# Linear-attention and recurrence projections in three split fp32r products, values of four heads in one pass, first recurrence tile ahead of the last head

## The chip, the cores and the metric

The program runs on one core of a Trainium2 chip. A core has a matrix engine (TensorE, PE; the loading of its weights is PEld), a vector engine (VectorE, DVE), an activation engine (ScalarE, ACT), a general engine (GpSimd, POOL) and a queue engine (SyncE, SP) that issues transfers. Each runs its own list of instructions; they wait for one another by semaphores. The metric is the device time of one execution in microseconds.

## The reference, cut to what matters

The program computes two blocks of a network for 512 positions of width 1024, in fp32. The change lies in the mixer of the first block, in its linear-attention heads and its gated recurrence:

```
def hgrn2_chunked(q, k, v, log_f):      # 8 heads of 128; S_t = diag(f_t) S_{t-1} + k_t v_t^T ; o_t = S_t^T q_t
...
def hybrid_mixer(u, lb, w_in, b_in, ...):
    proj = u @ w_in + b_in
    hq, hf, hi, hg, lx, lg, ca, cb, g_a, g_b, g_c = jnp.split(proj, cuts, axis=-1)
    q = jax.nn.silu(hq.astype(f32)).reshape(hshape)
    z = hf.astype(f32).reshape(hshape)
    f = lb_h + (1.0 - lb_h) * jax.nn.sigmoid(z)
    k = (1.0 - lb_h) * jax.nn.sigmoid(-z)
    v = hi.astype(f32).reshape(hshape)
    o_hg = hgrn2_chunked(q, k, v, jnp.log(f))
    y_hg = rmsnorm(o_hg, hg_norm)... * jax.nn.silu(hg)
    xb = causal_dwconv(lx, lru_conv_w, lru_conv_b)       # 4 taps
    ...                                                  # two gates from xb, a linear scan over positions
    y_lru = h.astype(u.dtype) * jax.nn.gelu(lg)
    cu = ca * jax.nn.sigmoid(cb)
    cu = causal_dwconv(cu, cv_dw_w, cv_dw_b)             # 31 taps
    y_cv = jax.nn.silu(layernorm(cu, cv_ln_g, cv_ln_b))
    merged = sigmoid(g_a) * (y_hg @ w_branch[0]) + sigmoid(g_b) * (y_lru @ w_branch[1]) + sigmoid(g_c) * (y_cv @ w_branch[2])
    return merged @ w_out
```

## The kernel before, in words

All activations lie with channels on the 128 partitions and the 512 positions along a row: xn is the normalised input of the mixer, 8 tiles of 128 channels. Weights come from memory as slabs of 128 x 1024 (512 KB) in one fixed order, by SyncE, into a ring of four; a slab's place is filled again once TensorE has counted it in slab_used.

A product is made in one of two ways. Plain (L515, L524, L532, L792): one fp32 matmul for each of the 8 input tiles, straight from ring and xn. Split (product, L220 to L222): weights and input are each the sum of a high part (what fp32r holds) and a low part, and low x high, high x high and high x low are added in PSUM. The high part of a slab is a copy on ScalarE (split_hi, L205, into whi), the low part a subtraction on GpSimd (split_lo, L210, in place in the ring as ring_r). The input's high part is xh1 (ScalarE), its low part xn_r (VectorE, x_lo_tile L233 or L926). The feed-forward parts and the merge are split; linear attention and recurrence are plain.

Linear attention (hgrn) goes head by head, each engine with a function of its own, over a hardware loop (Fori). Per head TensorE projects the query into bank 0, the output gate into bank 1, z into bank 2 and the values, position tile by position tile, into bank 3 (L532, with the bias by a one-row matmul L530). Its order is proj(h+1), inner part of h (hgrn_intra: L563 transposes, L555 eight score products, L571 states, L578 and L580 output, L583 sum of squares), query(h+2). ScalarE: sigmoid of the gate (L612), absolute value, exponentials and logarithms of z (L614 to L632), copy L634, sigmoid of the next query (L606), then square L638, logarithm L640 and exponential L642 for the norm. VectorE: gate L662, z L664, values copy L666, decays L670 to L684, level differences L690 and L691, masked queries and keys L699 and L700, score copies L707 and L712, states, next query L656, norm L728 and L730. Bank 1 is free for the next head's gate when L662 has run, and L662 waits for a sigmoid that waits for L730 of the head before.

The recurrence stage (lru) goes over 8 channel tiles. Per tile TensorE makes four projections (L792, banks 0 to 3) and two gate products (L802); VectorE does 4 taps (L888, L891), the convolution's input (L893), the gelu (L897 to L901), 31 taps (L913, L914, L920, two running sums in turn), the sum L922, and the scan (L928 to L932). Here 2 steps of the taps are independent of each other, while L891, L907 to L909 and L928 to L932 each wait for the step before. In the last tile ScalarE and VectorE also make xh1 and xn_r for the merge (L855, L926), and GpSimd splits the first merge slabs.

After it comes a layer norm (L813 mean, L939, L942, L870, L819) and the merge.

Of the kernel before, what the change touches and what calls it, by code (L numbers as in the profile page):

```python
# [7 lines left out]
ALU = mybir.AluOpType  # L8
# [6 lines left out]
P = 128  # L15
# [33 lines left out]
PARTS = [("ffn1_in", 2 * FT), ("ffn1_out", FT), ("hgrn", 4 * HEADS), ("lru", 4 * DT), ("merge", 6 * DT),  # L49
# [13 lines left out]
for _n, _c in PARTS:  # L63
    if _n in ("ffn1_in", "ffn1_out", "ffn2_in", "ffn2_out", "merge", "mix_out", "in2", "v2", "merge2", "out2"):
        SPLIT_AT[_n] = _at
        _at += _c
# [31 lines left out]
def hybrid_block_kernel(nc, stream, par, x_t, vbias, gate_w, masks, ctx_t, rpb, router_w, lora, experts, spill, xs_dram, ys_dram, out):  # L98
    ctx = ExitStack()
    with ctx:  # L100
# [46 lines left out]
        WHI = {"in2": whi2, "v2": whi2, "merge2": whi3, "out2": whi3}  # L147
        y_hg, y_lru, y_cv, merged = (big[:, i, :, :] for i in range(4))
# [325 lines left out]
        hq, hgl, hz, hlf, hk, hB, hqd, hkd, hv_tok, hkdT, hsc, hst, ho, hl1, he1, hEB = (WU(21 + n) for n in range(16))  # L474
        hst3 = hst[:, 0:3 * P].rearrange("p (c v) -> p c v", v=P)
        hi = Steps(sem("hgrn_pe"), "kdt s0 s1 kv s2 s3 s4 s5 s6 s7 o ss", 12)
        ha = Steps(sem("hgrn_act"), "sgg az e l1 sn e1 l2 EB Ekd E0 E1 kdT sgq osq lnss rstd", 16)
        hv = Steps(sem("hgrn_dve"), "gh z V lf t1 zc lf2 kh B dk " + " ".join(f"dr{i} dl{i}" for i in range(7))
                   + " qd kd " + " ".join(f"qm{i} km{i}" for i in range(7))
                   + " c0 c1 S1 S2 S3 c2 c3 c4 c5 c6 c7 qh y1 y2")  # L480
        hv.base = len(hv.names)
        hz_ready = sem("hgrn_zeros")
        vb_in = sem("vb_in")
        vb = shared[0:1, 11 * P:11 * P + D]
# [3 lines left out]
        xs_zeroed = sem("xs_zeroed")  # L488

# [5 lines left out]
        def hgrn_pool(pool):  # L495
# [7 lines left out]
            pool.memset(kl, 0.0).then_inc(hz_ready, 1)  # L503

        first_head = lambda h: isinstance(h, int) and h == 0

        def hgrn_query(pe, h, j0, i):

            if not first_head(h):
                pe.wait_ge(hv.sem, hv.at(h - 2, "qh"))  # L510
            w = use_slab(pe, "hgrn", j0, i, 4)
            for k in range(DT):
                if first_head(h):
                    pe.wait_ge(xn_ready, DT + k + 1)
                ins = pe.matmul(psum[:, 0, :], w[:, k, :], xn[:, k, :], start=k == 0, stop=k == DT - 1)  # L515
            ins.then_inc(slab_used, 1)

        def hgrn_proj(pe, h, j0, i):

            for n, (bank, freed) in enumerate(((1, "gh"), (2, "z"))):  # L520
                pe.wait_ge(hv.sem, hv.at(h - 1, freed))
                w = use_slab(pe, "hgrn", j0 + 1 + n, i, 4)
                for k in range(DT):
                    ins = pe.matmul(psum[:, bank, :], w[:, k, :], xn[:, k, :], start=k == 0, stop=k == DT - 1)  # L524
                ins.then_inc(slab_used, 1)

# [31 lines left out]
        def hgrn_intra(pe, h):  # L558
            pe.wait_ge(hv.sem, hv.at(h, "kd"))
# [39 lines left out]
        def hgrn_act(act):  # L599
# [8 lines left out]
            def head(h, last):  # L608
# [26 lines left out]
                if not last:  # L635
                    query(h + 1, 1)
# [2499 lines left out]
```

## Time and profile before

| what | us |
|---|---|
| median of 3 runs | 3611.16 (3605.09 to 3613.73) |
| span of the profiled execution, first to last instruction | 3608.5 |
| the same execution's time around the span | not listed apart; the median of the runs is 2.7 above the span |
| linear attention, first product to last L730 | 418.8 to 809.8 |
| recurrence stage, first product to last L932 | 809.9 to 1105.8 |
| mean granted TensorE clock over the span | 0.916 |

The engines' busy time is to be read by stage: from 500 to 768 us (six heads) TensorE is busy 248.0 of 268, VectorE 156.8, ScalarE 144.2, GpSimd 0. From 843 to 1069 (seven recurrence tiles) VectorE is busy 213.1 of 226. In a row of the order of time, a group of instructions stands with its start, its length from first start to last end, and in brackets how long the engine was idle before it and what ended that.

### The profile page before, as it was taken

The page shows a single profiled execution, that of the slowest core. Times are in us where ns is not written, and L with a number is a line of the kernel's source. Part 1 is how long each engine was busy: PE and PEld are TensorE (multiplying, and loading weights), DVE is VectorE, ACT ScalarE, POOL GpSimd, SP SyncE. Part 2 cuts the span into 40 slices and gives each one's busy share as a digit, 9 for nine tenths or more (in the row PEclk, how much of TensorE's full clock was granted, in tenths as well). Part 3 has the DMA queues.
Part 4 walks back from the last instruction along what each step waited for, and adds up shares of the span by engine and source line. Part 5 has one row for each costly group of instructions (what it writes and reads, how often), then busy time and mean ns, then how long its engine had stood idle before and what let it go on. Part 6 is the DMA issues. An engine that isn't in the chain of part 4 may idle for free.

```text
span 3608.5 us, 57604 instructions
## 1 busy us (share of the span) xinstructions
PE 3203.3 (89%) x22992; PEld 2391.1 (66%) x22992; DVE 1692.7 (47%) x2566; ACT 1336.9 (37%) x1755; POOL 766.0 (21%) x438
## 2 busy tenths in 40 slices
PE   7999999969967999899998999976777699599996
PEld 5887666644425887787833786756777477378885
DVE  2110155556996332311014403456666431489996
ACT  4432245553333322443122222222222232278884
POOL 4444200000004443444401231001111244200001
PEclk9999999989988999999999996557999889799998
DMA  2222511102211222222364121000000022399996
GB/s 103 95 95 89 210 52 46 47 24 74 74 50 53 94 94 87 77 93 87 97 230 141 53 85 38 12 9 3 4 4 4 2 88 94 129 362 412 412 412 270
DMA packets 106923, 397.17 MB, mean 110 GB/s; under 512 B 11680, under 2 KB 11696, under 8 KB 106240
## 3 DMA queue, kind: packets, MB, share of 16 engines
q1 hardware_dynamic: 95040, 347.42, 26.7%
q0 software_dynamic: 8400, 35.15, 2.6%
q10 hardware_dynamic: 3312, 12.06, 0.8%
q8 instruction: 139, 2.28, 0.3%
q14 instruction: 32, 0.26, 0.0%
HBM read 361.55 MB, written 33.03 MB: 109 GB/s over the span
## 4 chain that ended last, share of the span: by engine, by line
PE 66%; DVE 13%; issue 5%; ACT 2%; DMA 1%; DVEq 1%; POOL 0%; ACTq 0%; SPq 0%
PE psum L222 9%; PE psum L221 9%; PE psum L220 9%; PE psum L1760 6%; PE psum L2616 3%; PE psum L2617 3%; PE psum L2618 3%; PE psum L524 3%; PE psum L1429 2%; PE psum L1110 2%; DVE mem L920 2%; PE psum L532 2%; PE psum L1409 2%; PE psum L1790 1%; PE psum L792 1%
## 5 line engine op out<-in xcount | busy, mean ns | idle before, releaser
L210 POOL TENSOR_TENSOR ring_r<-ring,whi 128x1024 fp32r<-128x1024 f32 x247 | 600.0, 2439 | 1018.5 <-ACT whi L205 1018.5
L205 ACT ACTIVATE whi<-ring 128x1024 fp32r<-128x1024 f32 x247 | 255.6, 1055 | 529.6 <-DMA ring<-stream 529.4
L222 PE MATMUL psum<-xn_r,whi 128*128 128x512 f32 x1024 | 406.2, 397 | 0.0
L1760 PE MATMUL psum<-mem 64*64 64x64 f32 x9664 | 264.5, 234 | 87.9 <-DVE mem L2075 60.2
L1760 PEld LDWEIGHTS psum<-mem 64*64 64x64 f32 x9664 | 249.7, 147 | 100.9 <-DVE mem L2075 67.3
L2553 DVE TENSOR_TENSOR er_r<-er,eh 128x1024 fp32r<-128x1024 f32 x268 | 309.4, 1220 | 1.1 <-ACT eh L2541 0.5
L220 PE MATMUL psum<-ffn_xh,ring_r 128*128 128x512 f32 x704 | 279.7, 397 | 18.9 <-DVE xn_r L233 18.9
L2541 ACT ACTIVATE eh<-er 128x1024 fp32r<-128x1024 f32 x268 | 268.4, 1070 | 41.6 <-DMA er<-experts 40.9
L221 PE MATMUL psum<-ffn_xh,whi 128*128 128x512 f32 x704 | 281.3, 400 | 0.0
L792 PE MATMUL psum<-xn,ring 128*128 128x512 f32 x512 | 224.6, 599 | 8.5 <-DVE mem L730 4.3
L222 PEld LDWEIGHTS psum<-xn_r,whi 128*128 128x128 f32 x1024 | 193.9, 189 | 45.2
L220 PE MATMUL psum<-xh,ring_r 128*128 128x512 f32 x504 | 205.1, 407 | 9.1 <-DVE resid_r L1166 8.6
L221 PE MATMUL psum<-xh,whi 128*128 128x512 f32 x504 | 202.1, 401 | 0.0
L455 DVE TENSOR_TENSOR gu<-gu,psum 128x512 f32<-128x512 f32 x44 | 30.3, 688 | 358.4 <-ACT gu L434 358.4
L792 PEld LDWEIGHTS psum<-xn,ring 128*128 128x128 f32 x512 | 98.0, 192 | 134.0 <-issue 128.9
L220 PEld LDWEIGHTS psum<-ffn_xh,ring_r 128*128 128x128 f32 x704 | 132.9, 189 | 56.6 <-issue 19.7
L920 DVE SCALAR_TENSOR_TENSOR mem<-mem,pv 128x512 f32 (+1 forms) x232 | 157.1, 752 | 0.0
L221 PEld LDWEIGHTS psum<-ffn_xh,whi 128*128 128x128 f32 x704 | 133.4, 189 | 31.2
L220 PE MATMUL psum<-hid_hi,ring_r 128*128 (+1 forms) x352 | 143.9, 409 | 7.7 <-DVE hid_lo L459 7.7
L2616 PE MATMUL psum<-er_r,xbh 128*128 128x512 f32 x368 | 146.4, 398 | 3.4 <-DVE er_r L2553 2.0
L2618 PE MATMUL psum<-eh,xbl 128*128 128x512 f32 x368 | 144.4, 392 | 0.0
L2617 PE MATMUL psum<-eh,xbh 128*128 128x512 f32 x368 | 144.3, 392 | 0.0
(510 smaller groups left out, 6129.4 us busy)
## 6 DMA issues: line engine op xcount, KB each, us to landing
ring<-stream SPq DMA_DIRECT2D x359, 512.0 KB, 3.5
er<-experts SPq DMA_DIRECT2D x276, 512.0 KB, 8.0
xs_dram<-zero_row POOLq DMA_DIRECT2D x1, 12288.0 KB, 38.7
xs<-xs_dram SPq DMA_DIRECT2D x23, 512.0 KB, 8.1
ys_dram<-y_t ACTq DMA_DIRECT2D x23, 512.0 KB, 6.6
mem<-rpb POOLq DMA_DIRECT2D x8, 512.0 KB, 4.3
resid<-x_t SPq DMA_DIRECT2D x1, 2048.0 KB, 7.9
spill<-resid POOLq DMA_DIRECT2D x1, 2048.0 KB, 10.3
```

Of the source, the lines that this page charges most:

```text
L205: act.activation(WHI.get(part, whi)[:, (SLAB_AT[part] + j) % RING, :, :], w, ACT.Copy).then_inc(w_hi, 1)
L210: pool.tensor_tensor(ring_r[:, s, :, :], ring[:, s, :, :], f(WHI.get(part, whi)[:, s, :, :]), ALU.subtract).then_inc(w_lo, 1)
L220: pe.matmul(bank, lo[:, b, :], x_hi_, start=start, stop=False, skip_group_check=True)
L221: pe.matmul(bank, hi[:, b, :], x_hi_, start=False, stop=False, skip_group_check=True)
L222: return pe.matmul(bank, hi[:, b, :], x_lo_, start=False, stop=stop, skip_group_check=True)
L792: ins = pe.matmul(psum[:, bank, :], w[:, k, :], xn[:, k, :], start=k == 0, stop=k == DT - 1)
L1760: ins = pe.matmul(psum[o, bank, n * L:(n + 1) * L], lhs(n)[r], rhs(n)[r], start=i == 0 if start is None else start, stop=i == len(terms) - ...
L2541: act.activation(eh[:, SLOT[kind] + j, :], er[:, SLOT[kind] + j, :], ACT.Copy).then_inc(e_hi, 1)
L2553: dve.tensor_tensor(er_r[:, at, :], er[:, at, :], f(eh[:, at, :]), ALU.subtract).then_inc(e_lo_dve, 1)
L2616: pe.matmul(bank, x_hi_, lo_[:, cols], start=start, stop=False, skip_group_check=True)
L2617: pe.matmul(bank, x_hi_, hi_[:, cols], start=False, stop=False, skip_group_check=True)
L2618: return pe.matmul(bank, x_lo_, hi_[:, cols], start=False, stop=stop, skip_group_check=True)
```

## The change

1. The query, gate and z projections of all heads and the four projections of every recurrence tile become split products. Their slabs get a high and a low part (ScalarE L205, GpSimd L210 before; L209 and L214 in the new file), in a buffer whi_h of their own. xh1 and xn_r are made right at the mixer's norm, between the steps of norm_dve, and kept through both stages.
2. The values of four heads are made in one pass, split, with the weights as the moving side: two passes hv0 and hv1 of 96 matmuls into banks 4 to 7, one before head 0's projections and one after. VectorE adds the bias (values), for all 128 partitions. The slab order of the stream follows.
3. On ScalarE the gate's sigmoid of head h+1 stands right behind the query's sigmoid, with two buffers in turn (hgl), followed by an explicit load of the table set with logarithm and exponential. The next head's weight copies follow, ahead of the square.
4. The first recurrence tile's four projections (lru_first) stand before the last head's inner part.
5. In the recurrence loop ScalarE copies and GpSimd subtracts the next tile's four slabs (ahead).
6. The low parts for the merge leave the last recurrence tile; buffers move (y_cv, merged, y_cv_lo, mrg_lo).

```diff
-PARTS = [("ffn1_in", 2 * FT), ("ffn1_out", FT), ("hgrn", 4 * HEADS), ("lru", 4 * DT), ("merge", 6 * DT),
+PARTS = [("ffn1_in", 2 * FT), ("ffn1_out", FT), ("hv0", 4), ("hq0", 3), ("hv1", 4),
+         ("hgrn", 3 * HEADS - 3), ("lru", 4 * DT), ("merge", 6 * DT),
...
@@ hgrn_pool, after the two memsets
+            for j in range(4):
+                split_lo(pool, "hv0", j)
+            for j in range(3):
+                split_lo(pool, "hq0", j)
+            for j in range(4):
+                split_lo(pool, "hv1", j)
+            for h in range(1, HEADS):
+                for n in range(3):
+                    split_lo(pool, *head_slab(h, n))
+            for j in range(4):
+                split_lo(pool, "lru", j)
...
+        def hgrn_product(pe, bank, h, n):
+            w = use_split(pe, *head_slab(h, n))
+            for k in range(DT):
+                ins = product(pe, psum[:, bank, :], w, k, xh1[:, k, :], xn_r[:, k, :], k == 0, k == DT - 1)
+            ins.then_inc(slab_used, 1)
...
+        def hgrn_values(pe, g):
+            for s in range(4):
+                w_high, w_low = use_split(pe, f"hv{g}", s)
+                for c in range(4):
...
+                        pe.matmul(psum[:, 4 + c, :], xh1[:, k, at], w_low[:, cols, :], start=k == 0, stop=False, skip_group_check=True)
+                        pe.matmul(psum[:, 4 + c, :], xh1[:, k, at], w_high[:, cols, :], start=False, stop=False, skip_group_check=True)
+                        ins = pe.matmul(psum[:, 4 + c, :], xn_r[:, k, at], w_high[:, cols, :], start=False, stop=k == DT - 1,
...
@@ hgrn_pe
-            with pe.Fori(0, HEADS - 2) as h:
-                hgrn_proj(pe, h + 1, 4, h)
+            hgrn_values(pe, 0)
+            hgrn_query(pe, 0)
+            hgrn_proj(pe, 0)
+            hgrn_values(pe, 1)
+            hgrn_query(pe, 1)
+            for h in range(HEADS - 2):
+                hgrn_proj(pe, h + 1)
                 hgrn_intra(pe, h)
+                hgrn_query(pe, h + 2)
+            hgrn_proj(pe, HEADS - 1)
             hgrn_intra(pe, HEADS - 2)
+            lru_first(pe)
             hgrn_intra(pe, HEADS - 1)
@@ hgrn_act
+            def gate(h, count):
                 proj_done(act, h, 2)
-                act.wait_ge(hv.sem, hv.at(h - 1, "y2"))
-                act.activation(hgl, psum[:, 1, :], ACT.Sigmoid, bias=b(3)).then_inc(s, 1)
+                act.wait_ge(hv.sem, hv.at(h - 2, "y2"))
+                act.activation(hgl[h % 2], psum[:, 1, :], ACT.Sigmoid, bias=b(3, h)).then_inc(s, count)
...
                 if not last:
                     query(h + 1, 1)
+                    gate(h + 1, 1)
+                    act.preload_act_table_set("natural_log_exp_and_others")
+                if h < HEADS - 2:
+                    for n in range(3):
+                        split_hi(act, *head_slab(h + 2, n))
+                if h == HEADS - 2:
+                    for j in range(4):
+                        split_hi(act, "lru", j)
...
@@ lru_pool
-            with pool.Fori(0, DT) as j:
+            with pool.Fori(0, DT - 1) as j:
                 pool.wait_ge(lp.sem, lp.at(j - 1, "i"))
                 pool.dma_start(gwt, gate_w[:, j, :, :]).then_inc(gw_in, 16)
+                for n in range(4):
+                    split_lo(pool, "lru", 4 + n, j, 4)
...
@@ lru_act, channels
+                ahead = (lambda n: split_hi(act, "merge", n)) if last else (lambda n: split_hi(act, "lru", 4 + n, j, 4))
+                ahead(0)
+                ahead(1)
                 done(4)
...
+                ahead(2)
...
+                ahead(3)
...
@@ lru_dve, channels
-                if last:
-                    for k in range(DT):
-                        dve.wait_ge(x_hi, INPUT_AT["mix"] + k + 1)
-                        dve.tensor_tensor(xn_r[:, k, :], xn[:, k, :], f(xh1[:, k, :]), ALU.subtract).then_inc(x_lo, 1)
...
-            norm_dve(dve, 1, "norm_mix", xn)
+            norm_dve(dve, 1, "norm_mix", xn, xh1, "mix")
```

ScalarE in one head of linear attention, before (L612 sigmoid of the gate, L614 to L624 the functions of z):

```order
L612 ACT_TABLE_LOAD [waits hgrn_dve]
L612 ACTIVATE mem<-psum,pv 128x512 [waits slab_used]
L614 ACTIVATE mem<-mem 128x512 [waits hgrn_dve]
L616 ACT_TABLE_LOAD
L616 ACTIVATE mem<-mem 128x512 [waits hgrn_act]
L618 ACT_TABLE_LOAD
L618 ACTIVATE mem<-mem,ones 128x512 [waits hgrn_act]
L620 ACT_TABLE_LOAD
L620 ACTIVATE mem<-mem 128x512 [waits hgrn_dve]
L622 ACTIVATE mem<-mem 128x512 [waits hgrn_dve]
L624 ACT_TABLE_LOAD
L624 ACTIVATE mem<-mem,ones,lb 128x512 [waits hgrn_act]
```

ScalarE from the sigmoid of the next query to the first functions of z, now (L642 and L647 the two sigmoids, L209 weight copies, L687 to L691 the norm, L652 and L654 what L614 and L616 were):

```order
L642 ACT_TABLE_LOAD [waits hgrn_pe]
L642 ACTIVATE mem<-psum,pv 128x512 [waits slab_used]
L647 ACTIVATE mem<-psum,pv 128x512 [waits hgrn_dve,slab_used]
L679 ACT_TABLE_LOAD
L209 ACTIVATE whi_h<-ring 128x1024 [waits slab_in0]
L209 ACTIVATE whi_h<-ring 128x1024 [waits slab_in1]
L209 ACTIVATE whi_h<-ring 128x1024 [waits slab_in2]
L687 ACTIVATE mem<-psum 128x512 [waits hgrn_pe]
L689 ACTIVATE mem<-psum,eps 128x512 [waits hgrn_pe]
L691 ACTIVATE mem<-mem 128x512 [waits hgrn_act]
L652 ACTIVATE mem<-mem 128x512 [waits hgrn_dve]
L654 ACTIVATE mem<-mem 128x512 [waits hgrn_act]
```

The table loads between the functions of z are gone, and one load and three weight copies of 128 x 1024 now stand ahead of the square.

GpSimd between the first feed-forward and the merge, before (two memsets, then those of the recurrence stage and its loop, which only fetches gate weights):

```order
L502 MEMSET mem 128x3584 [waits resid_ready]
L503 MEMSET mem 128x3584
L772 MEMSET mem 128x3 [waits hgrn_dve]
L773 MEMSET mem 128x30
L774 UNCONDITIONAL_BRANCH
L774 ISA
L776 ISA [waits lru_pe]
```

and now (the same memsets; L214 is the weight subtraction, 36 of them in linear attention, and from L843 the recurrence loop):

```order
L513 MEMSET mem 128x3584 [waits resid_ready]
L514 MEMSET mem 128x3584
L214 TENSOR_TENSOR ring_r<-ring,whi_h 128x1024 [waits w_hi] x36
L841 MEMSET mem 128x3 [waits hgrn_dve]
L842 MEMSET mem 128x30
L843 UNCONDITIONAL_BRANCH
L843 ISA
L845 ISA [waits lru_pe]
L845 DMA mem<-gate_w 128x256
L213 ISA
L214 TENSOR_TENSOR ring_r<-ring,whi_h 128x1024 [waits w_hi]
```

36 subtractions moved into linear attention, and the recurrence loop has four in each of its seven rounds.

## Rows read from the trace of the kernel before

**Rows 1.** The page, part 1: busy us (share) and instructions of each engine.
```profile
PE 3203.3 (89%) x22992; PEld 2391.1 (66%) x22992; DVE 1692.7 (47%) x2566; ACT 1336.9 (37%) x1755; POOL 766.0 (21%) x438
```

**Rows 2.** Busy time by stage; columns: stretch, length, engines, PEclk, DMA share, GB/s.
```profile
843.00:1069.00 226.00, 203.91 (x471) 88.84 (x470) 213.14 (x323) 80.17 (x99) 3.77 (x7) 0.97 0.21 69
```

**Rows 3.** Order of time (start us, length us, what), GpSimd, VectorE, TensorE, linear attention.
```profile
414.89 3.08 POOL L503 MEMSET mem<- 128x3584 f32 x1
...
417.89 5.39 DVE L367 SCALAR_TENSOR_TENSOR xn<-resid,pv,std 128x512 f32<-128x512 f32 x8
...
418.79 9.08 PE L515 MATMUL psum<-xn,ring 128*128 128x512 f32 x16 [5.14 <-DVE xn L367]
...
481.21 0.60 PE L563 MATMUL psum<-ident,mem 128*128 128x128 f32 x4
...
498.70 0.69 DVE L730 TENSOR_TENSOR mem<-mem 128x512 f32 x1
...
766.76 0.69 DVE L730 TENSOR_TENSOR mem<-mem 128x512 f32 x1
```

**Rows 4.** Order of time, TensorE: split products, then two plain slabs.
```profile
37.08 0.40 PE L221 MATMUL psum<-ffn_xh,whi 128*128 128x512 f32 x1
...
37.31 0.39 PE L222 MATMUL psum<-xn_r,whi 128*128 128x512 f32 x1
...
427.71 13.90 PE L524 MATMUL psum<-xn,ring 128*128 128x512 f32 x32
```

**Rows 5.** Order of time in one head, ScalarE, TensorE, VectorE.
```profile
592.51 0.63 ACT L614 ACTIVATE mem<-mem 128x512 f32<-128x512 f32 x1 [1.59 <-DVE mem L664]
...
593.16 1.28 ACT L616 ACT_TABLE_LOAD   x1
...
615.24 0.41 DVE L700 TENSOR_TENSOR mem<-mem 128x256 f32<-128x256 f32 x1
...
628.99 7.03 PE L515 MATMUL psum<-xn,ring 128*128 128x512 f32 x16
```

**Rows 6.** Order of time at the end of head 7, VectorE and ScalarE; last, one group of ScalarE.
```profile
793.85 0.68 DVE L707 COPY mem<-psum 128x512 f32<-128x512 f32 x1
...
801.13 0.72 DVE L712 COPY_PREDICATED mem<-ident,psum 128x512 f32<-128x512 uint32 x1 [0.18 <-DVE mem L712]
...
803.77 0.60 ACT L638 ACTIVATE mem<-psum 128x512 f32<-128x512 f32 x1 [12.67 <-PE psum L580]
...
808.34 0.75 DVE L728 SCALAR_TENSOR_TENSOR mem<-psum,pv,mem 128x512 f32<-128x512 f32 x1 [6.49 <-ACT mem L642]
...
L606 ACT ACTIVATE mem<-psum,pv 128x512 f32<-128x512 f32 x8 | 5.5, 687 | 0.1
```

**Rows 7.** Order of time in the recurrence stage, VectorE; last ScalarE.
```profile
842.60 0.75 DVE L893 SCALAR_TENSOR_TENSOR mem<-psum,pv,mem 128x512 f32<-128x512 f32 x1 [17.25 <-ACT mem L835]
...
912.17 0.69 DVE L901 SCALAR_TENSOR_TENSOR mem<-mem 128x512 f32<-128x512 f32 x1 [0.69 <-ACT mem L842]
...
1068.37 0.74 DVE L893 SCALAR_TENSOR_TENSOR mem<-psum,pv,mem 128x512 f32<-128x512 f32 x1
...
1075.56 1.99 ACT L205 ACTIVATE whi<-ring 128x1024 fp32r<-128x1024 f32 x2
```

**Rows 8.** Single lines, duration ns min/median/max, and the stretch of GpSimd beside them.
```profile
L210 POOL TENSOR_TENSOR ring_r<-ring,whi x66: 2333/2411/2436, 22.5 to 389.4; 128x1024 fp32r<-128x1024 f32 x66
...
1076.68 10.49 POOL L210 TENSOR_TENSOR ring_r<-ring,whi 128x1024 fp32r<-128x1024 f32 x2 [36.24 <-ACT whi L205]
...
L210 POOL TENSOR_TENSOR ring_r<-ring,whi x2: 2779/5261/7743, 1076.7 to 1084.4; 128x1024 fp32r<-128x1024 f32 x2
...
L909 DVE SCALAR_TENSOR_TENSOR mem<-mem x8: 691/692/2711, 860.0 to 1082.3; 128x512 f32<-128x512 f32 x8
...
L920 DVE SCALAR_TENSOR_TENSOR mem<-mem,pv x29: 739/740/2833, 1072.3 to 1096.9; 128x512 f32<-128x512 f32 x29
...
L942 DVE TENSOR_TENSOR mem<-mem x8: 1526/1760/2832, 1108.1 to 1119.7; 128x512 f32<-128x512 f32 x8
```

More of the change, by code:

```diff
@@ L577, in hgrn_intra @@
                 s = slice(c * P, (c + 1) * P)
-                ins = pe.matmul(psum[:, 4, s], hv_tok[:, s], hsc[:, s], start=True, stop=c == 0)
+                ins = pe.matmul(psum[:, 4, s], value(c), hsc[:, s], start=True, stop=c == 0)
                 if c:
@@ L642, in head @@
                 act.activation(hl1, hl1, ACT.Exp, scale=-0.5).then_inc(s, 1)
-            query(0, 4)
-            with act.Fori(0, HEADS - 1) as h:
-                head(h, False)
-            head(HEADS - 1, True)
+            split_hi(act, "hv0", 0)
+            split_hi(act, "hv0", 1)
+            x_hi_act(act, 1, xh1)
+            split_hi(act, "hv0", 2)
+            split_hi(act, "hv0", 3)
+            for n in range(3):
+                split_hi(act, *head_slab(0, n))
+            split_hi(act, "hv1", 0)
+            query(0, 1)
+            split_hi(act, "hv1", 1)
+            gate(0, 4)
+            act.preload_act_table_set("natural_log_exp_and_others")
+            split_hi(act, "hv1", 2)
+            split_hi(act, "hv1", 3)
+            for h in range(HEADS):
+                head(h)
         def hgrn_dve(dve):
@@ L729, in head @@
                 own("y1")
-                dve.tensor_tensor(y_hg[:, h, :], hl1, hgl, ALU.mult).then_inc(s, 1)
+                dve.tensor_tensor(y_hg[:, h, :], hl1, hgl[h % 2], ALU.mult).then_inc(s, 1)
+            values(0)
             query(0, 3)
-            with dve.Fori(0, HEADS - 1) as h:
-                head(h, False)
-            head(HEADS - 1, True)
+            for h in range(HEADS):
+                head(h)
         lxp = work[:, 0:520]
@@ L795, in lru_proj, with lru_first @@
                     lru_gates(pe, gates)
+        def lru_first(pe):
+            for bank, head, freed in ((0, HEADS - 2, "qh"), (1, HEADS - 1, "gh"), (2, HEADS - 1, "z"), (3, HEADS - 1, "z")):
+                pe.wait_ge(hv.sem, hv.at(head, freed))
+                w = use_split(pe, "lru", bank)
+                for k in range(DT):
+                    ins = product(pe, psum[:, bank, :], w, k, xh1[:, k, :], xn_r[:, k, :], k == 0, k == DT - 1)
+                ins.then_inc(slab_used, 1)
         def lru_gates(pe, j):
@@ L850, in channels @@
                 act.activation(la_t, lr, ACT.Exp, scale=c).then_inc(s, 1)
-                if last:
-                    split_hi(act, "merge", 0)
-                    split_hi(act, "merge", 1)
-                    for k in range(DT):
-                        act.activation(xh1[:, k, :], xn[:, k, :], ACT.Copy).then_inc(x_hi, 1)
                 act.wait_ge(lv.sem, lv.at(j, "w"))
@@ L3072, in lay_out @@
     mix = k_slabs(i["w_in_mix"][0]).reshape(11, DT, P, SLAB, P)
-    parts.append(mix[[0, 3, 1, 2]].transpose(1, 0, 2, 3, 4).reshape(-1, P, SLAB, P))
+    heads = mix[[0, 3, 1]].transpose(1, 0, 2, 3, 4).reshape(-1, P, SLAB, P)
+    values = i["w_in_mix"][0][:, 2048:3072].reshape(4, 2, P, 2, 4, P).transpose(3, 0, 2, 1, 4, 5).reshape(2, 4, P, SLAB, P)
+    parts.extend([values[0], heads[0:3], values[1], heads[3:]])
     parts.append(mix[[4, 5, 6, 7]].transpose(1, 0, 2, 3, 4).reshape(-1, P, SLAB, P))
```

131 lines of the change are left out of this document (69 added, 62 removed).

## The prediction

> **What bounds the kernel now.** I read the page first: over the whole span TensorE is busy 89%, VectorE 47%, GpSimd 21% [rows 1]. That average hides the two stages that the change touches, so I went on to the busy time by stage, then to the order of time of each engine inside one head and inside one channel tile, and last to single instructions of GpSimd and VectorE. The reader is to see four things.
>
> Linear attention runs in a loop in which TensorE closes the cycle. The last VectorE step of a head (L730) ends at 499.4 us for head 0 and 767.4 for head 6 [rows 3], so a head takes 268.1 / 6 = 44.7 us, and TensorE is at work nearly all of it: three projections, the values product and the inner part of the previous head stand in one row.
>
> The recurrence stage is bound by VectorE: from 843 to 1069 us it is busy 213.1 of 226, GpSimd 3.8 [rows 2]. The step that takes the convolution input (L893) is at 842.60 for tile 0 and 1068.37 for tile 7 [rows 7]; in a steady tile VectorE waits about 0.7 us (L901).
>
> The only idle stretch of VectorE is at the start of that stage: L893 of tile 0 waits 17.3 us for the projections [rows 7].
>
> GpSimd and VectorE hinder each other. A weight subtraction on GpSimd takes 2.41 us when VectorE is quiet (66 of them in the first feed-forward). In the last recurrence tile there are two, and they took 7.74 and 2.78 us, while one L909 took 2.71 instead of 0.69 and one L920 2.83 instead of 0.74: 2.0 and 2.1 us lost on VectorE [rows 8]. The first subtraction was issued in a gapless row of L920 and did not get through for 5 us; it came in where a VectorE step waits for the one before it (L907 to L909).
>
> **Part by part.** All sums are against the profiled span of 3608.5 us; the median of the runs shown is 2.7 us above it, and I add that at the end.
>
> *Cheaper projections.* Plain: two slabs (16 products) in 13.90 us, or 0.86 us each. Split: one matmul each 0.23 us (37.08 to 37.31), three to a product, 0.70 us, so 5.6 us a slab instead of 6.9 [rows 4]. Of a head's 44.7 us three plain slabs are 20.8; the other 24 are the values and the inner part. The values (32 narrow products with their bias rows, the columns of one more slab and some on top) are an estimated 9.6 of them; they now go in two passes of 96 matmuls, 22.4 us each, for all heads, outside the loop. What is left to TensorE in a head is 3 x 5.6 and an inner part of 14: 31 us. That is not what is to be had, since another chain comes to the front.
>
> *Start of linear attention.* TensorE began at 418.79, as soon as the first normalised tile was there [rows 3]. Now it needs that tile's low part and the first split weight slab. GpSimd's two memsets end at 418.0, VectorE's row of 8 L367 begins at 417.89 [rows 3], and with the 8 low parts put between them it runs gapless to about 428 (8 x 0.67 from the row of 5.39, and 8 x 0.6 for the low parts, an estimate from L730, a step of the same kind and size, 0.69 less 0.09 of overlap). By rows 8 the subtraction waits for its end: TensorE starts near 430 (+11.5). If GpSimd gets in at once it is 422.7 (+4): that is the other end. From there to head 0's inner part (L563, 481.21 before, 62.4 us after the start) now stand 14 slabs, 14 x 5.6 = 78.3 us, plus about 2 us in which TensorE starts slower after a pause (before, the first slab took 9.08 instead of 7.03 us [rows 3, 5]), plus 4 us in which head 1's first slab waits for its subtraction behind VectorE's gapless row, plus 1.5 for the pause that this makes: 86. The inner part starts 35 us later.
>
> *A head's new cycle.* From VectorE's L730: gate and z steps 1.5; then L614 to the last L700, 592.51 to 615.65 = 23.1, less three table loads of 1.28 on the path that the preload takes away (L616, L618, L624) = 19.4; the score copies 793.85 to 801.85 = 8.0 [rows 6] (head 7, where TensorE had nothing else to do); then on ScalarE a sigmoid table load 1.28, two sigmoids 1.3, the preload 1.3, three weight copies 3.0 (two take 1.99 [rows 7]) before the square (L638) can run: it starts 6.1 us after the last score copy instead of 1.9; then square, sum, logarithm, exponential and two VectorE steps, 6.2 us before [rows 6] less two loads that partly lay beside TensorE: 4.9. Sum 1.5 + 19.4 + 8.0 + 6.1 + 4.9 = 39.9. GpSimd's three subtractions begin after the first weight copy and last 7.2 us; the third still runs when L730 (two operands in SBUF) is issued: 1.1 us. 41.0 a head, 3.7 less than 44.7; TensorE (31) is then hidden. Against y of head 0 (+35, and a tail 4 us longer than before by the same items: +39), six heads give back 22: +17 at the end of head 6. Head 7, with the first recurrence tile (22.4 us of TensorE) filling the wait of head 7's own chain, gives back 4: +13.
>
> The Trainium skill (ScalarE: Activation LUTs, "What ACT_TABLE_LOAD costs") gives a switch of sets 1.28 us of load and 1.38 us of drain. The load agrees; the trace does not show the drain: L616's load starts at 593.16, right behind L614, which ends at 593.14 [rows 5]. By the page a head would gain some 4 us more, 28 us in all.
>
> *First recurrence tile ahead.* L893 of tile 0 came 32.8 us after linear attention's end (809.8). Now its products are done: table load and copy 2.5, three filter taps 3.8, sigmoid meanwhile: 7.1. Gain 25.7: the sum stands at -13.
>
> *Weight splits in the recurrence stage.* 28 slabs (tiles 1 to 7) are now copied on ScalarE and subtracted on GpSimd inside the stage that VectorE bounds. ScalarE's 4 x 1.0 us lie in waits of 5 to 10 us a tile and cost nothing. Each subtraction costs VectorE 2.05 us [rows 8] or, if it falls into the one idle 0.7 us, less: 4 x 2.05 - 0.7 = 7.5 us a tile, seven tiles 52.5. Below, nothing (all of them find gaps); above, 4 x 2.8 = 11. I take 7.5, since the only two subtractions seen in this very loop cost that. The sum so far is +40. Cheaper projections gain nothing here; TensorE goes from 29 to 24 us in a tile of 39.
>
> The Trainium skill (SBUF — State Buffer, "Who interferes with whom") states that a VectorE instruction with two SBUF inputs and a GpSimd instruction that reads SBUF exclude each other for a whole instruction. The trace agrees: L909 and L920 have two inputs in SBUF and were held for 2.0 and 2.1 us. Without such a lock the whole sum would be -15, which is the first rival below.
>
> *Last tile and merge.* The eight low parts leave VectorE's last tile (4.9 us), but TensorE's mean product there did not wait for them. The high parts start 5 us earlier, and fewer of L942's eight steps (1.76 us instead of 0.69 beside GpSimd [rows 8]) are hit: -2. The moved buffers and the wider bias transfer cost nothing.
>
> Sum: 39 (start) - 22 - 4 - 25.7 + 52.5 - 2 = +37.8 us. Span 3646, run 3649 us; I say 3648, as the items are not sharper than that.
>
> **Rivals.**
> *The lock does not bite.* Subtractions find the seams between VectorE's steps and the recurrence tile stays at 31.8. For: GpSimd's other 66 ran undisturbed; against: there VectorE was mostly idle, and the two in this loop did bite. Then 37.8 - 52.5 = -15, and with a start at 422.7 a further -8: 3588 to 3599 us, faster. It decides if a subtraction costs VectorE under 0.7 us.
> *Starved GpSimd.* The subtractions wait 5 us each as the first did, TensorE waits for the slabs, gates come late: 4 x 5.3 = 21 us of GpSimd a tile would still fit, but two waits in a row in front of the gates would give tiles near 46: +50 more, 3698.
> *TensorE still closes the head.* If the head chain were shorter than I read, heads would fall to 31: another -60 us, 3588. Against: every item of the 41 has its row.
> *Half and half.* Some subtractions hit and some not: about 3620, no change.
>
> **Chances.** Forecast 0.62 (its own range 3625 to 3675), lock without effect 0.20, starved 0.08, TensorE-bound heads 0.03, half and half 0.07. A run of this kernel tells about 0.3% (11 us) from no change. Slower 0.70, same 0.08, faster 0.22. Range 3588 to 3690.
>
> **What would show it.** Single L920 and L891 near 2.8 us, four GpSimd subtractions a tile and a tile distance of 39 us confirm the main term; a distance of 32 refutes it and the forecast. TensorE's first product at 430 or 423 settles the start. Head distance 41, with VectorE's longest wait on the exponential behind the weight copies, confirms the head chain; 31 to 36 says that I put too much on ScalarE. The convolution input of tile 0 should come 7 us after linear attention's end.

## The result, and the profile after

The kernel became slower, by less than 1%: 3639.2 us (median of 4 runs, 3631.3 to 3644.2) against 3610.9 us for the kernel before (median of 4). The ratio is 1.0085, with a 95% interval of 1.0067 to 1.0104. The profiled execution has a span of 3642.3 us, 33.8 more than before. The forecast was 3648 us, +37.8 in the span. The profiled execution is the slowest of the four: in the medians the difference is 28.4 us.

Busy time of the engines over the whole span, then the two stages by stretch (length, PE, PEld, DVE, ACT, POOL, PEclk, DMA share, GB/s):

```profile
PE 3151.6 (87%) x23056; PEld 2478.8 (68%) x23056; DVE 1753.7 (48%) x2566; ACT 1327.4 (36%) x1763; POOL 930.8 (26%) x502
...
532.00:780.00 248.00, 194.01 (x973) 158.70 (x973) 153.74 (x361) 107.79 (x127) 43.33 (x20) 0.91 0.12 39
828.00:1107.00 279.00, 195.77 (x694) 145.27 (x692) 269.38 (x324) 106.72 (x126) 85.90 (x35) 0.82 0.18 56
```

TensorE has 52 us less to do than in [rows 1], and the kernel is slower all the same. In the recurrence stage it is now busy for 70% of the time, while VectorE is busy for 269 of 279 us: the stage [rows 2] went from 226 to 279 us. VectorE computes nothing new there; its steps only last longer.

The start of linear attention, in order of time (start us, length us):

```profile
417.33 5.08 POOL L214 TENSOR_TENSOR ring_r<-ring,whi_h 128x1024 fp32r<-128x1024 f32 x2
...
417.28 6.34 DVE L371 SCALAR_TENSOR_TENSOR xn<-resid,pv,std 128x512 f32<-128x512 f32 x3
...
424.37 0.77 PE L559 MATMUL psum<-ring_r,xh 128*128 128x512 f32 x1 [11.33 <-DVE xn_r L237]
...
512.20 0.60 PE L596 MATMUL psum<-ident,mem 128*128 128x128 f32 x4
```

GpSimd's first two subtractions got in at once, and it was VectorE that waited: three normalisation steps took 6.34 us, where eight took 5.39 before [rows 3]. TensorE therefore began at 424.4, 5.6 us later than before, and the inner part of head 0 31 us later.

The heads: the last VectorE step of a head, L800 (it was L730), then ScalarE's chain in front of it in head 2, and L800 of head 6:

```profile
L800 DVE TENSOR_TENSOR mem<-mem x8: 693/936/2292, 532.4 to 817.7; 128x512 f32<-128x512 f32 x8
...
603.86 1.28 ACT L642 ACT_TABLE_LOAD   x1 [11.55 <-PE psum L585]
605.15 0.69 ACT L642 ACTIVATE mem<-psum,pv 128x512 f32<-128x512 f32 x1
605.74 0.68 ACT L647 ACTIVATE mem<-psum,pv 128x512 f32<-128x512 f32 x1
606.43 1.28 ACT L679 ACT_TABLE_LOAD   x1
607.73 2.95 ACT L209 ACTIVATE whi_h<-ring 128x1024 fp32r<-128x1024 f32 x3
610.58 0.57 ACT L687 ACTIVATE mem<-psum 128x512 f32<-128x512 f32 x1
...
780.56 2.29 DVE L800 TENSOR_TENSOR mem<-mem 128x512 f32<-128x512 f32 x1
```

Head 0 ends at 532.4 and head 6 at 780.6, so a head takes 248.2 / 6 = 41.4 us instead of 44.7 (41.9 the first, 41.2 to 41.4 the others). All of linear attention still ends 8.6 us later than before (last step at 817.7 against 809.1), since head 0 ends 33.7 us later. The square L687 starts 6.76 us after the start of the last score copy (603.82), 6.0 after its end: a load, two sigmoids, a load and three weight copies stand in front of it.

The recurrence stage: the convolution input L971 (it was L893), one steady tile, and the end of the last tile:

```profile
828.13 0.74 DVE L971 SCALAR_TENSOR_TENSOR mem<-psum,pv,mem 128x512 f32<-128x512 f32 x1
...
911.69 0.74 DVE L971 SCALAR_TENSOR_TENSOR mem<-psum,pv,mem 128x512 f32<-128x512 f32 x1
...
926.19 17.03 DVE L998 SCALAR_TENSOR_TENSOR mem<-mem,pv 128x512 f32<-128x512 f32 x16
...
947.32 4.40 DVE L969 SCALAR_TENSOR_TENSOR mem<-mem,pv 128x512 f32<-128x512 f32 x3
951.64 0.74 DVE L971 SCALAR_TENSOR_TENSOR mem<-psum,pv,mem 128x512 f32<-128x512 f32 x1
...
929.99 8.05 POOL L214 TENSOR_TENSOR ring_r<-ring,whi_h 128x1024 fp32r<-128x1024 f32 x3 [13.01 <-ACT whi_h L209]
948.34 2.83 POOL L214 TENSOR_TENSOR ring_r<-ring,whi_h 128x1024 fp32r<-128x1024 f32 x1 [10.31 <-ACT whi_h L209]
...
1106.97 0.74 DVE L971 SCALAR_TENSOR_TENSOR mem<-psum,pv,mem 128x512 f32<-128x512 f32 x1
...
1134.78 0.69 DVE L1006 SCALAR_TENSOR_TENSOR mem<-mem 128x512 f32<-128x512 f32 x1
```

Tile 0 has its input at 828.1, 14.5 us earlier than in [rows 7]; tile 7 at 1107.0, 38.6 later. A tile takes 40.0 us instead of 31.8. In it GpSimd runs three subtractions beside a row of 16 filter taps, which takes 17.03 us (10.68 in a kernel without them, below), and one beside a row of three, which takes 4.40 (2.54): 6.35 + 1.86 = 8.2 us, the whole difference.

### The profile page after: what moved, and what is told of

Read it like the earlier page. It is cut to its first block, busy times and chain, and to the rows that moved or that the text cites. A ratio compares the mean times of both kernels' runs of the same rounds, so it can differ in the third digit from the quotient of the medians.

```text
span 3642.3 us, 57318 instructions
## 1 busy us (share of the span) xinstructions
PE 3151.6 (87%) x23056; PEld 2478.8 (68%) x23056; DVE 1753.7 (48%) x2566; ACT 1327.4 (36%) x1763; POOL 930.8 (26%) x502
## 4 chain that ended last, share of the span: by engine, by line
PE 72%; DVE 15%; issue 7%; ACT 3%; DMA 1%; POOL 1%; DVEq 0%; ACTq 0%; SPq 0%; POOLq 0%
PE psum L224 13%; PE psum L226 13%; PE psum L225 13%; PE psum L1834 6%; PE psum L2690 4%; PE psum L2691 3%; PE psum L2692 3%; PE psum L1503 2%; PE psum L1184 2%; DVE mem L998 2%; PE psum L1483 2%; PE psum L1864 1%; PE psum L585 1%; PE psum L1492 1%; DMA ring<-stream 1%
## 5 line engine op out<-in xcount | busy, mean ns | idle before, releaser
L214 POOL TENSOR_TENSOR ring_r<-ring,whi 128x1024 fp32r<-128x1024 f32 x247 | 595.1, 2421 | 999.6 <-ACT whi L209 999.6
L224 PE MATMUL psum<-xh,ring_r 128*128 128x512 f32 x952 | 405.8, 426 | 57.2 <-POOL ring_r L214 38.8
L209 ACT ACTIVATE whi<-ring 128x1024 fp32r<-128x1024 f32 x247 | 255.6, 1055 | 531.1 <-DMA ring<-stream 530.9
L2615 ACT ACTIVATE eh<-er 128x1024 fp32r<-128x1024 f32 x268 | 268.3, 1071 | 41.0 <-DMA er<-experts 40.3
L214 POOL TENSOR_TENSOR ring_r<-ring,whi_h 128x1024 fp32r<-128x1024 f32 x64 | 171.2, 2697 | 409.2 <-ACT whi_h L209 409.2
L224 PEld LDWEIGHTS psum<-xh,ring_r 128*128 128x128 f32 x952 | 189.0, 199 | 118.1 <-POOL ring_r L214 47.2
L998 DVE SCALAR_TENSOR_TENSOR mem<-mem,pv 128x512 f32 (+1 forms) x232 | 190.9, 897 | 0.0
L225 PE MATMUL psum<-xh,whi_h 128*128 128x512 f32 x448 | 189.2, 422 | 0.0
L226 PE MATMUL psum<-xn_r,whi_h 128*128 128x512 f32 x448 | 186.7, 417 | 0.0
```

The lines of the kernel that those rows point to most:

```text
L209: act.activation(WHI.get(part, whi)[:, (SLAB_AT[part] + j) % RING, :, :], w, ACT.Copy).then_inc(w_hi, 1)
L214: pool.tensor_tensor(ring_r[:, s, :, :], ring[:, s, :, :], f(WHI.get(part, whi)[:, s, :, :]), ALU.subtract).then_inc(w_lo, 1)
L224: pe.matmul(bank, lo[:, b, :], x_hi_, start=start, stop=False, skip_group_check=True)
L225: pe.matmul(bank, hi[:, b, :], x_hi_, start=False, stop=False, skip_group_check=True)
L226: return pe.matmul(bank, hi[:, b, :], x_lo_, start=False, stop=stop, skip_group_check=True)
L998: dve.scalar_tensor_tensor(half_sum, cup[:, t:t + T], tap("cv_w", t), half_sum, ALU.mult, ALU.add).then_inc(s, 1)
```

## The experiments

Each ratio is to the kernel before, with its 95% interval. A time "after" is of the changed kernel.

**Recurrence tiles 1 to 7 plain again.**

```diff
-                for n in range(4):
-                    split_lo(pool, "lru", 4 + n, j, 4)
...
-                    ins = product(pe, psum[:, bank, :], w, k, xh1[:, k, :], xn_r[:, k, :], k == 0, k == DT - 1)
+                    ins = pe.matmul(psum[:, bank, :], w[:, k, :], x_whole[:, k, :], start=k == 0, stop=k == DT - 1)
...
+            for k in range(DT):
+                pool.tensor_tensor(x_whole[:, k, :], f(xn_r[:, k, :]), f(xh1[:, k, :]), ALU.add).then_inc(x_sum, 1)
```

> Tiles 1 to 7 of the recurrence stage multiply the plain fp32 weights again, with no weight splits (28 copies on ScalarE and 28 subtractions on GpSimd gone); GpSimd puts the input together again once (8 additions beside head 7). Theory (the subtractions hold VectorE, about 8 us a tile): the distance of two tiles falls from 40.0 to 31.8 us and the kernel by some 53 us, to 3586 (3580 to 3594, where the 8 additions hit VectorE). Rival (the tile became longer because of the slower TensorE clock or of the order of the slabs): plain products need 29 us of TensorE a tile instead of 24, and the distance stays above 36: 3610 or more.

3592.2 us (7 runs, 3580.4 to 3596.0), ratio 0.995 (0.9933 to 0.9967). Span 3590.4, 51.9 less than after. VectorE in order of time, tile 2 to tile 3, and the starts of L975 (the convolution input) in all tiles:

```profile
907.21 10.68 DVE L1002 SCALAR_TENSOR_TENSOR mem<-mem,pv 128x512 f32<-128x512 f32 x16
...
921.99 2.54 DVE L973 SCALAR_TENSOR_TENSOR mem<-mem,pv 128x512 f32<-128x512 f32 x3
...
L975 DVE SCALAR_TENSOR_TENSOR mem<-psum,pv,mem x8: 744/745/747, 824.0 to 1055.4; 128x512 f32<-128x512 f32 x8
```

The tile is back at 31.8 us, and tile 7's input comes 51.6 us earlier. The rival (slower TensorE clock, order of slabs) is out: plain products need more of TensorE, and the tile is shorter. Linear attention ends as after (817.3), and tile 0's input now comes 6.7 us behind it instead of 10.4: the splits for tile 1 had already held tile 0's first taps.

**Four more subtractions in the kernel before, and four memsets in their place.**

```diff
+                for n, step in enumerate(("lx", "lx", "sb", "sqg")):
+                    pool.wait_ge(la.sem, la.at(j, step))
+                    pool.wait_ge(extra, 4 * j + n)
+                    pool.tensor_tensor(spare, other, other, ALU.subtract).then_inc(extra, 1)
...
(second kernel)
+                    pool.memset(spare, 0.0).then_inc(extra, 1)
```

> The kernel before with four more GpSimd subtractions (128x1024 fp32, result unused) in each of the recurrence tiles 0 to 6, and nothing else: no weight copies, the products plain. Theory (the subtractions alone make the tile longer): the distance of two tiles goes from 31.8 to 39.3 to 40.0 us, the kernel takes some 55 us more, 3665. Rival (part of the 8.2 us a tile is due to ScalarE's copies, or to slabs that come late): the distance stays at 32 to 36, 3610 to 3640.

> The same places as in the kernel with four more subtractions, but each is a memset of 128x1024 fp32: GpSimd writes SBUF and reads nothing. Theory (what holds VectorE is a GpSimd instruction that reads SBUF): distance 31.8 us, time as before, 3609. Rival (any long GpSimd instruction on SBUF holds VectorE): 36 to 40 us, 3640 to 3665.

With subtractions 3651.6 us, ratio 1.0113 (1.0097 to 1.013); with memsets 3614.6, ratio 1.0001 (0.9987 to 1.0015). First the kernel with subtractions: taps, the second row with its subtraction, the next tile's input, GpSimd beside the taps; all starts of the input. Then GpSimd and the starts of the input with memsets.

```profile
938.00 15.59 DVE L930 SCALAR_TENSOR_TENSOR mem<-mem,pv 128x512 f32<-128x512 f32 x16
...
957.72 4.27 DVE L901 SCALAR_TENSOR_TENSOR mem<-mem,pv 128x512 f32<-128x512 f32 x3
...
940.83 6.91 POOL L783 TENSOR_TENSOR mem<-resid 128x1024 f32<-128x1024 f32 x3 [12.38 <-ACT mem L842]
...
L903 DVE SCALAR_TENSOR_TENSOR mem<-psum,pv,mem x8: 743/747/751, 843.2 to 1108.5; 128x512 f32<-128x512 f32 x8
```

```profile
L783 POOL MEMSET mem<- x28: 952/952/1049, 821.9 to 1034.3; 128x1024 f32 x28
...
L903 DVE SCALAR_TENSOR_TENSOR mem<-psum,pv,mem x8: 744/745/751, 842.6 to 1068.1; 128x512 f32<-128x512 f32 x8
```

Subtractions alone, with TensorE's work and ScalarE's left as they were, lengthen a tile by 6.6 us (4.9 in the row of 16, 1.7 in the row of three) and the seven distances by 39.6. The direction is the theory's, the size is not: I expected 7.5 to 8.2 a tile and 3665 us. These subtractions read one buffer twice and last 2.15 us (median), those of the changed kernel read two and last 2.8 beside taps; the former hold a row of taps for 1.6 us each (4.91 / 3), the latter for 2.1 (6.35 / 3). The two kinds also write different types, and which of these differences makes the price is not shown. The 28 memsets cost nothing (31.8 us a tile). They are shorter too, 0.95 us, but even at half the price of a subtraction they would have shown as 3 us a tile, and no filter tap beside one lasts over 0.75 us. So for steps with two inputs in SBUF, as the taps are, it is the reading of SBUF that counts.

**The subtractions on VectorE.**

```diff
+                ahead = (lambda n: None) if last else (lambda n: split_lo(dve, "lru", 4 + n, j, 4))
...
+                ahead(0)
+                ahead(1)
                 own("cu")
```

> The changed kernel with the 28 subtractions of the recurrence tiles on VectorE itself instead of GpSimd. Theory: VectorE pays its own time, about 1.3 us each (twice the 0.69 of a 512-column step with two SBUF inputs) instead of 2.05 us of being held: 31.8 + 4 x 1.3 - 0.7 = 36.3 us a tile, 7 x 3.7 = 26 us less, 3613. Rival (copies on ScalarE come too late for the fixed places and VectorE waits for them): 38 us or more a tile, 3625 or more.

3653.2 us, ratio 1.0112 (1.0093 to 1.0131); a tile takes 41.0 to 41.6 us, and the last distance is 44.9 (35.5 with the subtractions on GpSimd). VectorE's two first subtractions of a tile, and its steps behind the first taps:

```profile
910.32 2.36 DVE L214 TENSOR_TENSOR ring_r<-ring,whi_h 128x1024 fp32r<-128x1024 f32 x2
...
927.25 0.69 DVE L982 TENSOR_TENSOR mem<-mem 128x512 f32<-128x512 f32 x1 [2.84 <-ACT mem L928]
...
929.90 0.70 DVE L984 TENSOR_TENSOR mem<-mem 128x512 f32<-128x512 f32 x1 [1.95 <-ACT mem L933]
```

My theory falls. The subtraction costs what I said (1.2 us), but it now stands in VectorE's order behind the convolution input, the gate products stand behind two split slabs on TensorE, and VectorE waits 2.84 + 1.95 us for the gates: 4 x 1.2 + 4.8 = 9.6 us a tile, more than the 8.2 on GpSimd. The rival's time came true, but not its cause: VectorE waits in front of none of the 28 subtractions, so ScalarE's copies are never late.

**Tile 0 behind head 7.**

```diff
-            lru_first(pe)
             hgrn_intra(pe, HEADS - 1)
...
             pe.wait_ge(hv.sem, hv.end(HEADS))
+            lru_first(pe)
```

> The projections of recurrence tile 0 stand behind head 7 again instead of ahead of its inner part. Theory (the move alone is worth the idle time of VectorE at the start of the stage): 22.4 us of TensorE come back onto the path, less what head 7 gains without them (about 2): 3660. Rival (they delay head 7 as much as they save): no change, 3640.

3657.3 us, ratio 1.0136 (1.0118 to 1.0153), 18 us more than after; 3660 was expected. End of head 7 and tile 0's input:

```profile
816.39 0.69 DVE L799 TENSOR_TENSOR mem<-mem 128x512 f32<-128x512 f32 x1
...
843.64 0.75 DVE L971 SCALAR_TENSOR_TENSOR mem<-psum,pv,mem 128x512 f32<-128x512 f32 x1 [11.33 <-ACT mem L918]
```

The input comes 27.3 us behind head 7, against 33.5 before and 10.4 after. So of the 23.0 us between before and after, 6.2 come from the cheaper products and 16.8 from the move. Head 7 ends only 1.3 us earlier without it: what fills its waits costs it almost nothing.

**The weight copies of a head at its end.**

```diff
-                if h < HEADS - 2:
-                    for n in range(3):
-                        split_hi(act, *head_slab(h + 2, n))
                 ...
                 act.activation(hl1, hl1, ACT.Exp, scale=-0.5).then_inc(s, 1)
+                if h < HEADS - 2:
+                    for n in range(3):
+                        split_hi(act, *head_slab(h + 2, n))
```

> In heads 0 to 5 ScalarE's three weight copies for the head after next stand behind the exponential that ends the head, not ahead of the square. Theory (ScalarE's copies stand in the chain that sets a head): a head falls from 41.2 to about 38 us, the last step of head 6 comes 18 us earlier and the kernel takes about 3620. Rival (the copies' place costs nothing, since TensorE or the next head's slabs set the pace; the subtractions then fall into VectorE's gapless rows and the slabs come late): a head stays at 41 or more, 3639 or above.

3634.1 us, ratio 1.0072 (1.0053 to 1.009): 5 us less than after where I expected 19 (in the profiled spans 10); the intervals of the two ratios overlap, so the gain of the whole kernel is not clear of noise. The first five heads take 39.6 us each (530.7 to 728.6), but the sixth takes 44.0: the four copies for the recurrence, which the edit leaves ahead of its square, stand in the chain, and the held steps come on top. Head 2: the square, GpSimd, and two VectorE steps of the next head; then the second of these lines in all heads, here and in the changed kernel.

```profile
605.43 0.60 ACT L684 ACTIVATE mem<-psum 128x512 f32<-128x512 f32 x1
...
609.62 7.85 POOL L214 TENSOR_TENSOR ring_r<-ring,whi_h 128x1024 fp32r<-128x1024 f32 x3 [31.44 <-ACT whi_h L209]
...
615.25 2.77 DVE L739 SCALAR_TENSOR_TENSOR mem<-mem 128x512 f32<-128x512 f32 x1
...
L739 DVE SCALAR_TENSOR_TENSOR mem<-mem x8: 692/2758/2787, 474.8 to 779.1; 128x512 f32<-128x512 f32 x8
```

```profile
L739 DVE SCALAR_TENSOR_TENSOR mem<-mem x8: 691/691/693, 474.2 to 787.0; 128x512 f32<-128x512 f32 x8
```

The square starts 3.9 us after the last score copy (601.52) instead of 6.76: the copies did stand in the chain, with 2.9 us. But the subtractions now fall on L737 and L739, which have two inputs in SBUF and last 1.68 and 2.77 us instead of 0.69: 3.1 us given back. That most heads are still 1.6 to 2.0 us shorter comes from TensorE. From the first masked score copy to the last it is 6.5 us instead of 7.4, with a granted clock of 1.00 where it was 0.87 (629.3 to 641.5 here, 632.6 to 645.8 after), and the pair of sums behind the square is mostly shorter (last section). The first part need not be the edit's: in the kernel with the subtractions on VectorE, whose heads are those of the changed kernel, it is also 6.5 us in four of six heads, and these take 40.3. I had named this rival only as slabs that come late; it is the same lock. The same edit together with the plain tiles:

> Both at once: the recurrence tiles 1 to 7 plain, and the weight copies of heads 2 to 7 behind the exponential. The two effects lie in different stages and should add: 3639 - 53 - 18 = 3568, faster than both kernels. Rival: if the head's copies cost nothing where they are, it is 3586 as with the plain tiles alone.

3582.9 us, ratio 0.993 (0.9907 to 0.9954), 9.2 us less than with plain tiles alone (span 12.7 less). The two parts add, and the copies are again worth half of what I expected: the first five heads took 39.4 us each, the sixth again 44.0.

**The weight copies early.** Plain tiles, and the three copies right behind the copy of the transposed key (in head 6 the four for the recurrence).

```diff
                 act.activation(hkdT, psum[:, 4, :], ACT.Copy).then_inc(s, 3 if last else 1)
+                if h < HEADS - 2:
+                    for n in range(3):
+                        split_hi(act, *head_slab(h + 2, n))
```

> Plain recurrence tiles, and in every head the weight copies for the head after next stand right behind the copy of the transposed key, where ScalarE waits 8 to 11 us for the last scores, so that GpSimd subtracts while VectorE copies scores out of PSUM. Theory (the lock takes two SBUF inputs on VectorE; score copies have one, the mask, beside PSUM): the chain is 3.9 us shorter as with the late copies and nothing is given back: 37.3 us a head, 3592 - 23 = 3569. Rival (score copies are held as well, about 2 us for each subtraction): the gain is eaten, a head takes 41 to 43 and the kernel 3590 to 3600.

3561.6 us, ratio 0.9862 (0.9846 to 0.9879). GpSimd beside the score copies of head 2, one of those copies, all copies, and the last step of all heads:

```profile
587.84 8.75 POOL L216 TENSOR_TENSOR ring_r<-ring,whi_h 128x1024 fp32r<-128x1024 f32 x3 [28.64 <-ACT whi_h L211]
...
594.04 0.74 DVE L787 COPY_PREDICATED mem<-shared,psum 128x512 f32<-128x512 uint32 x1 [0.38 <-DVE mem L787]
...
L787 DVE COPY_PREDICATED mem<-shared,psum x48: 724/739/755, 515.9 to 781.2; 128x512 f32<-128x512 uint32 x48
...
L805 DVE TENSOR_TENSOR mem<-mem x8: 691/692/694, 531.2 to 788.7; 128x512 f32<-128x512 f32 x8
```

A head takes 37.0 us (221.9 over six), as the theory had it. Not one of 48 score copies, with a mask in SBUF and scores in PSUM, lasts over 0.755 us, and subtractions run beside 45 of them; no L805 is held (here 0.69, after up to 2.29). The Trainium skill (SBUF — State Buffer, "Who interferes with whom") states just this: two SBUF inputs on VectorE contend with a GpSimd instruction that reads SBUF, not with one that only writes it, and a VectorE instruction with at most one SBUF input does not contend as long as it is outside the modes that use both ports. The runs agree in all three cases: 2.1, 0.0 and 0.0 us.

One kind of VectorE step with a single SBUF input was held all the same, the TENSOR_SCALAR; no row shows in which mode it ran. These are the first step of the gelu in the changed kernel (tile 0, beside subtractions) and in the kernel before with memsets (tile 0, beside a memset):

```profile
L975 DVE TENSOR_SCALAR mem<-mem x8: 408/410/1954, 828.8 to 1107.6; 128x512 f32<-128x512 f32 x8
```

```profile
L907 DVE TENSOR_SCALAR mem<-mem x8: 415/417/1255, 843.8 to 1068.8; 128x512 f32<-128x512 f32 x8
```

Beside a subtraction it took 1.5 us longer, beside a memset 0.8 us. Alone it takes 0.41 us, less than the 0.69 of a two-input step of the same size. So neither one input nor a GpSimd instruction that only writes is safe for this step.

**Two further edits on top.** First the table load behind the square; then, in a second kernel, also the gates of tile 0 first and the merge's subtractions behind the last tap.

```diff
-                    act.preload_act_table_set("natural_log_exp_and_others")
                 ...
                 act.activation(ho, psum[:, 4, :], ACT.Square).then_inc(s, 1)
+                if not last:
+                    act.preload_act_table_set("natural_log_exp_and_others")
```

> The kernel with plain tiles and early copies; in addition the table load that stands between the two sigmoids and the square in every head but the last comes behind the square. Theory (it stands in the chain of the head with its 1.28 us, and behind the square it lies beside TensorE's sum, for which ScalarE waits 1.5 us): a head takes 37.2 - 1.3 = 35.9 us, the kernel 9 us less than 3562, 3553. Rival (the square needs a load of its own, or the logarithm's load then comes late): 3562 or more.

> As with the load behind the square, and in the recurrence stage the gate products of tile 0 ahead of the projections of tile 1 (VectorE waits 5.1 us for them there) and GpSimd's two weight subtractions of the merge behind the last filter tap instead of beside it (two steps held by 2 us each). Theory: tile distance 0 to 1 falls from 36.9 to about 32.5, the last tile's 35.5 to 31.5: 8 us less, 3545. Rival (the projections of tile 1 come late by what the gates gain; the merge starts later by what the last tile gains): 3553.

Both take 3549.7 us, with ratios of 0.9831 (0.9816 to 0.9847) and 0.9829 (0.9815 to 0.9842). ScalarE in head 2 of the first; then tile 0's gates on TensorE and the last two steps of tile 7 on VectorE in the second.

```profile
595.01 0.60 ACT L691 ACTIVATE mem<-psum 128x512 f32<-128x512 f32 x1
595.63 1.28 ACT L693 ACT_TABLE_LOAD   x1
596.92 0.69 ACT L695 ACTIVATE mem<-psum,eps 128x512 f32<-128x512 f32 x1
```

```profile
783.21 3.75 PE L888 MATMUL psum<-mem 128*128 128x512 f32 x4 [9.15 <-DVE mem L976]
...
852.89 0.75 DVE L978 SCALAR_TENSOR_TENSOR mem<-psum,pv,mem 128x512 f32<-128x512 f32 x1
...
1037.78 3.25 DVE L1011 TENSOR_TENSOR_SCAN mem<-mem 128x512 f32<-128x512 f32 x1
1041.06 2.66 DVE L1013 SCALAR_TENSOR_TENSOR mem<-mem 128x512 f32<-128x512 f32 x1
```

The load now lies beside TensorE's sum and the square needs none of its own: a head takes 35.5 us. The last two edits gave nothing, as the rival said. Tile 1's input came 2.6 us nearer to tile 0's, but tile 2's stands 70.0 us behind tile 0's instead of 69.1: TensorE had idled 9.2 us ahead of the gates. The merge's subtractions left the taps and fell on the scan and the step behind it (3.25 and 2.66 us instead of 1.23 and 0.69).

## Why the prediction was right, point by point

The prediction held, and for its reason: the forecast of 3648 us was 0.2% high. Its terms miss by up to 5.3 us and partly cancel, so the closeness of the sum is in part luck. In the same clock readings:

| term | predicted | measured |
|---|---|---|
| end of head 0 | +39 | +33.7 |
| six heads | -22 | -19.9 |
| head 7 | -4 | -5.2 |
| first recurrence tile | -25.7 | -23.0 |
| splits in the recurrence stage | +52.5 | +53.1 |
| last tile and merge | -2 | -4.8 |
| sum | +37.8 | +33.9 |

The last row but one is what is left of the span behind tile 7's input, some 2540 us; it holds that stretch's scatter from run to run as well.

- *Splits.* The size fits, but by two errors that cancel. I charged seven tiles with 4 x 2.05 less 0.7 us of idle time, 7.5 each. In fact nothing falls into the idle time: six distances grew by 8.2 (4.0 us more in all), and the last, where only the merge's two subtractions run, by 4.1 (3.4 less). The plain-tile and the added-subtraction kernels show the cause. Without the 28 splits tile 7's input comes 51.6 us earlier, of which 3.8 lie ahead of tile 0's input.
- *Start.* This term was mis-sized by 5 us, most of it by one choice: "TensorE starts near 430". I let the only subtraction of [rows 8] that waited decide. Here the memset ended and the subtraction began 0.05 us after VectorE's row did, and GpSimd got in. TensorE began at 424.4, 1.7 us behind the other end that I had given (422.7), since two steps of VectorE's row were held by about 2.1 us each. From there to head 0's inner part it was 87.8 us (predicted 86), and the tail of head 0 grew by 2.7 us (predicted 4).
- *Head.* 41.0 was right for the steady head; the chain ran through the copies as described. Five of the six took 41.2 to 41.4 us, the first 41.9. Outside these six, L800 of head 6 was held for 1.6 us by the splits for the recurrence. How much of the shorter head is due to cheaper products and how much to the table loads taken out was not told apart.
- *Tile 0.* "7.1" us, counted from the end of head 7's last step, was near for a stage without splits (6.0 with plain tiles, 9.7 after; from the start of that step 6.7 and 10.4); I had overlooked that the splits for tile 1 start in tile 0's first microseconds. The parts of the gain were not told apart: 16.8 of it is the move.
- *Rivals.* "The lock does not bite" needed 32 us a tile: refuted. "Starved GpSimd" came true only in tile 0, where one subtraction took 8.9 us and the distance to tile 1 grew by no more than the others (8.3 us). No run shows heads at TensorE's own 31 us: in the changed kernel TensorE is busy for 78% of them, and the best kernel reached 35.5.

## What to carry to other kernels

Before work is moved to an idle GpSimd, list the operands of what VectorE does at that moment: beside steps with two SBUF inputs a GpSimd instruction that reads SBUF cost VectorE here most of its own duration (1.6 of 2.15 us, 2.1 of 2.8), beside steps that read PSUM it cost nothing, and a TENSOR_SCALAR step with one SBUF input was held even by a memset. So choose the place and not only the engine. Make products cheaper only where TensorE sets the pace: the same split lost 52 us in a stage that VectorE bounds, while the head of linear attention, whose pace TensorE had set, became 3.3 us shorter (together with the table loads taken out). When a step is taken out of a chain, check what it lands on; here 2.9 us saved brought 3.1 us of held steps one head later, and what the head still gained came from TensorE.

## What the runs showed of the hardware that was not expected

- A subtraction issued into a gapless row of two-input VectorE steps is kept out for very different times: at 417.33 GpSimd went in at once, while one in tile 0 of the changed kernel (issued at 850.28) took 8.9 us to end, and of the two in [rows 8] one took 7.7 and the other 2.8. What decides it was not settled. Once in, a row of subtractions keeps its turn: the three at 929.99 took 8.05 us.
- A shorter pause in a chain can pay twice where TensorE stands in it. These are the sums of squares (L616) of head 2 in the changed kernel, then of heads 2 and 5 with the copies late; the number behind POOL's is the granted clock:

```profile
611.20:613.20 2.00, 1.99 (x3) 0.96 (x4) 0.00 (x0) 0.00 (x0) 2.00 (x2) 0.50 0.00 0
```

```profile
606.00:607.20 1.20, 1.12 (x2) 0.30 (x2) 0.00 (x0) 0.03 (x1) 0.00 (x0) 1.00 0.00 0
724.40:726.40 2.00, 1.99 (x2) 0.42 (x2) 0.00 (x0) 0.00 (x0) 0.00 (x0) 0.53 0.00 0
```

  Behind 4.8 us without a product TensorE ran at 0.50, the level of 1.2 GHz, and the two products took 2.07 us, in heads 1 to 5 alike. Behind 2.0 us it was not one thing: in heads 2 and 4 it ran at 1.00, that of 2.4 GHz, and they took 1.13 us; in heads 1 and 3 they took 1.27 and 1.47, and in heads 0 and 5 2.0 us, mostly at the lower level. Behind 0.7 us, as in the kernel before, the pair took 1.12 us in every head. What decides between the levels behind 2.0 us was not settled.
- A table load of 1.28 us between a square and a logarithm is free if the square's result has TensorE's sum to wait for, and no drain beyond the load shows in these rows (595.63 + 1.28 = 596.91, and the logarithm starts at 596.92).
